# Building the place matrices of a PEER layer's gate stage on GpSimd instead of ScalarE

## The reference, cut to what matters

```python
act = jax.nn.gelu(jnp.einsum('thkd,td->thk', ub, xb), approximate=False)
vb = jnp.take(v, eb, axis=0)
return jnp.einsum('thk,thkd->td', gb * act, vb)
```

## Time and profile before

| what | value |
|---|---|
| time, median of 3 runs | 2997.28 us (2995.55 to 2999.19) |
| profiled execution, span from first to last instruction | 2998.2 us |
| profiled span against the median of the runs | 0.9 us longer |
| PE busy | 2734.9 us (91%) |
| DVE busy | 1819.1 us (61%) |
| ACT busy | 1457.1 us (49%) |
| POOL busy | 13.8 us (29 instructions) |
| mean granted TensorE clock | 0.94 of full speed |
| HBM traffic | 149 GB/s over the span |

### The profile page before, as it was taken

One profiled execution on the slowest core, in us unless ns is written; L12 is line 12 of the kernel. 1 busy time (PEld: TensorE's weight loads), 2 busy tenths in 40 slices (PEclk: granted clock), 3 DMA queues, 4 the chain that ended last, 5 costly groups with the idle time before them and its releaser, 6 DMA issues.

```text
span 2998.2 us, 47842 instructions
## 1 busy us (share of the span) xinstructions
PE 2734.9 (91%) x16426; PEld 2417.8 (81%) x16430; DVE 1819.1 (61%) x3134; ACT 1457.1 (49%) x2435; POOL 13.8 (0%) x29
## 2 busy tenths in 40 slices
PE   8889999977999997889999976899997998998898
PEld 6689999965888876579999965788876986866797
DVE  3456786499555553245778479655555656454564
ACT  4334444487454543334444477445444544553543
POOL 0000000000000000000000000000000000000000
PEclk9899999977999998789999987999998998998999
DMA  6245555500555553145555520455555554533454
GB/s 202 71 141 183 182 182 173 192 14 0 186 192 193 192 178 103 34 136 179 180 184 169 182 69 0 137 195 192 194 182 164 182 189 142 170 109 113 146 181 149
DMA packets 123982, 446.85 MB, mean 149 GB/s; under 512 B 14280, under 2 KB 14920, under 8 KB 123648
## 3 DMA queue, kind: packets, MB, share of 16 engines
q1 hardware_dynamic: 119808, 434.16, 44.0%
q0 software_dynamic: 2608, 9.08, 1.0%
q10 hardware_dynamic: 1488, 2.59, 0.2%
HBM read 444.74 MB, written 1.05 MB: 149 GB/s over the span
## 4 chain that ended last, share of the span: by engine, by line
PE 79%; DVE 13%; issue 4%; ACT 3%; DVEq 1%; DMA 0%; ACTq 0%
PE ps L621 38%; PE ps L593 12%; PE ps L599 12%; PE ps L596 12%; DVE SC L1750 3%; DVE big L1758 3%; DVE w_lo L337 1%; DVE SC L1400 1%; DVE X L1407 1%; DVEq L1750 1%; PE ps L571 1%; PE ps L818 1%; DVE tops L1694 1%; DVE big L1407 1%; DVE x_lo L1454 1%
## 5 line engine op out<-in xcount | busy, mean ns | idle before, releaser
L337 DVE TENSOR_TENSOR w_lo<-ring,w_hi 128x1024 fp32r<-128x1024 f32 (+1 forms) x808 | 986.2, 1221 | 917.8 <-ACT w_hi L330 907.0
L330 ACT CAST w_hi<-ring 128x1024 fp32r<-128x1024 f32 (+1 forms) x808 | 845.2, 1047 | 1115.8 <-PE ps L621 582.3
L593 PE MATMUL ps<-x_hi,w_hi 128*128 128x256 f32 x3136 | 775.4, 285 | 8.7 <-DVE x_lo L1459 4.4
L596 PE MATMUL ps<-x_lo,w_hi 128*128 128x256 f32 x3136 | 773.3, 284 | 0.0
L593 PEld LDWEIGHTS ps<-x_hi,w_hi 128*128 128x128 f32 x3136 | 605.0, 193 | 11.5 <-issue 10.4
L596 PEld LDWEIGHTS ps<-x_lo,w_hi 128*128 128x128 f32 x3136 | 605.3, 193 | 0.0
L599 PE MATMUL ps<-x_hi,w_lo 128*128 128x256 f32 x3136 | 443.3, 284 | 4.0 <-DVE w_lo L337 4.0
L621 PE MATMUL ps<-w_hi,x_hi 128*128 128x512 f32 x1488 | 417.8, 400 | 26.1 <-DVE x_lo L1454 12.6
L599 PEld LDWEIGHTS ps<-x_hi,w_lo 128*128 128x128 f32 x3136 | 405.7, 193 | 7.7 <-DVE w_lo L337 7.7
L621 PE MATMUL ps<-w_hi,x_lo 128*128 128x512 f32 x1488 | 409.8, 394 | 0.0
L621 PE MATMUL ps<-w_lo,x_hi 128*128 128x512 f32 x1488 | 407.9, 393 | 0.3 <-DVE w_lo L337 0.3
(11 more groups left out here) (221 smaller groups left out, 1512.5 us busy)
## 6 DMA issues: line engine op xcount, KB each, us to landing
ring<-in_u SPq DMA_DIRECT2D x256, 512.0 KB, 3.3
ring<-in_v SPq DMA_DIRECT2D x256, 512.0 KB, 3.2
ring<-in_ffn_in SPq DMA_DIRECT2D x88, 512.0 KB, 3.3
ring<-in_ffn_out SPq DMA_DIRECT2D x44, 512.0 KB, 3.3
ring<-in_wq SPq DMA_DIRECT2D x32, 512.0 KB, 3.3
ring<-in_ple_gate SPq DMA_DIRECT2D x16, 512.0 KB, 3.3
SC<-in_rows POOLq DMA_DIRECT2D x11, 512.0 KB, 4.4
ring<-in_a_qk SPq DMA_DIRECT2D x8, 512.0 KB, 4.5
```

Of the source, the lines that this page charges most:

```text
L330: nc.scalar.copy(part(w_hi, i)[:, used(name)], tile(i)[:, used(name)]).then_inc(tiles_hi, 1)
L337: nc.vector.tensor_tensor(part(w_lo, i)[:, at], tile(i)[:, at], part(w_hi, i)[:, at], ALU.subtract).then_inc(tiles_split, 1)
L593: mm = nc.tensor.matmul(bank(s)[:, 0:T], hi[:, k, :], x_hi[:, k, :], start=(k == 0), stop=False)
L596: nc.tensor.matmul(bank(s)[:, 0:T], hi[:, k, :], x_lo[:, k, :], start=False, stop=False)
```

## The change

GpSimd builds `place`, in a new function `places(layer)` in its own program. Two instructions do a group of four tokens: a subtraction with two inputs, `iota` repeated for each of four tokens and the four index columns repeated along 128 elements, into `distance` (128x512), and a comparison of that with zero into `place` (128x512). Between the two GpSimd waits on its own semaphore `distances`; from the fifth group on it waits for `slot_full` of group g - 4 ahead of the subtraction, as ACT did. `place` keeps its four buffers, its memory, and its values, zeros and ones. ACT's loop with five instructions per group is gone. `route_T[:, 1]` is now a plain copy of the index, where before it was multiplied by -1.

```diff
+            def places(layer):
+                gates = SLOT[f"gates{layer}"]
+                pool.wait_ge(routes_turned, layer + 1)
+                moved(pool, SLOT[f"last_u{layer}"], BODY)
+                for g in range(T // 4):
+                    k = g % 4
+                    if g >= 4:
+                        slot_here(pool, gates + g - 4)
+                    slots = route_T[:, 1, 4 * g:4 * g + 4]
+                    nc.gpsimd.tensor_tensor(distance[:, k], iota[:, None, :].to_broadcast([P, 4, P]),
+                                            slots[:, :, None].to_broadcast([P, 4, P]), ALU.subtract
+                                            ).then_inc(distances, 1)
+                    pool.wait_ge(distances, T // 4 * layer + g + 1)
+                    nc.gpsimd.tensor_scalar(place[:, k], distance[:, k], 0.0, None, ALU.is_equal
+                                            ).then_inc(place_rows, 1)
             load_rows(0, (gates_split, 1))
             load_rows(1, (routes_turned, 1))
+            places(0)
             load_p(0)
             load_rows(2)
             load_rows(3, (routes_turned, 2))
+            places(1)
             load_p(1)
...
-                def place_distances(k, turns):
-                    slot_here(act, gates + k - 4, turns)
-                    for t in range(4):
-                        ins = S.activation(distance[:, k, t], iota[:], ACT.Abs,
-                                           bias=route_T[:, 1, ds(turns * 16 + (4 * k + t), 1)])
-                    ins.then_inc(distances, 1)
-                def places(k, turns):
-                    act.wait_ge(distances, turns * 4 + (T // 4 * layer + k + 1))
-                    S.activation(place[:, k], distance[:, k], ACT.Relu, scale=-1.0, bias=1.0
-                                 ).then_inc(place_rows, 1)
...
                     if q == 0:
-                        ts(route_T[:, 1, :], bank(s)[:, T:2 * T], -1.0, None, ALU.mult)
+                        step(V.tensor_copy(route_T[:, 1, :], bank(s)[:, T:2 * T]))
```

## The result

The changed kernel takes 3041.94 us (median of 4 runs, 3041.5 to 3043.97) against 2996.5 us of the kernel before, timed beside it (4 runs, 2995.55 to 2999.19): 1.0158 times as long, 95% interval 1.0146 to 1.0171. It is slower, as forecast, but by 45 us and not by 188. One run of experiment 5 (3500.77 us) and one of experiment 7 (5338.7 us) were slow: their medians count them, their ratios don't.

The account below looks back on a forecast made before the run. DVE was taken to bound the gate stages at 2.23 us per group; 128 x (3.7 - 2.23) = +188 us took the span from 2998.2 to 3186, median 3185 us. Own range 3110 to 3265, 8-in-10 range 3015 to 3300.

Parts of the forecast that it names:

- What bounds the kernel before: Gate stages: DVE sets the pace at 2.23 us per group; removing ACT's 1.86 us gains nothing in the steady state.
- GpSimd's two instructions: Per group in the gate stages: subtraction 1.15, comparison 0.74, hop 0.13, alone 2.02 us, bounds 1.19 to 2.55.
- The step that failed: Gate stages: gate_group and GpSimd instructions exclude each other, apply_gates is free; 3.11 to 4.32 us per group, chance 0.63.
- The rule: Skill's shared-port rule for DVE and GpSimd in the gate stages: by it a group costs between 3.11 and 4.32 us.
- no exclusion, GpSimd too slow alone: Rival, gate stages: GpSimd's own cycle, at most 2.55 us, sets the pace; +41 us, 3038 us; chance 0.13.
- The signs that I had named: Gate stages, if right: apply_gates 3.1 to 4.3 us apart and unchanged in length, gate_group longer, PE waiting longer for gated_rows.
- The clock argument: Gate stages: PE's release starts the subtraction, beside gate_group at full clock, below apply_gates at lower clock; middle 3.7 us.
- The start of the stage: Before the first apply_gates: a faster first place could gain at most 3.3 us in both layers; first groups meet the block.
- The queues: GpSimd's in_p load stays at the stage's end, code readying hides behind the row loads, SP's queue is untouched: no cost.

Follow-up runs that it names:

- experiment 5: Changed kernel without the subtraction; GpSimd compares iota with each token's index column, four 128x128 comparisons per group: 3008.94 us, ratio 1.0034.
- experiment 7: Changed kernel with GpSimd's subtraction alone, no comparison, also waiting for DVE's gate_rows of group g-2: 3002.05 us, ratio 1.0025.
- experiment 8: Three-engine version of the changed kernel: GpSimd subtracts, lined up with apply_gates; ACT makes place and one weighted row of four, DVE three: 2968.29 us, ratio 0.9903.
- experiment 4: Changed kernel with a two-input product, distance times distance, in place of GpSimd's comparison: 3149.77 us, ratio 1.053.
- experiment 1: Changed kernel with one of DVE's four gate_group instructions per group, the other three left out: 3048.32 us, ratio 1.0187.
- experiment 2: Changed kernel with DVE's gate_group reading iota from a PSUM copy made once per layer: 3042.25 us, ratio 1.0169.
- experiment 6: Changed kernel with GpSimd's subtraction alone, written into place, no comparison, waiting only for PE's buffer: 3036.8 us, ratio 1.0135.

## Why the prediction was right in sign and wrong in size

- **What bounds the kernel before**: right. DVE at 2.23 us a group, and ACT's work off the path: with a quarter of `gate_group` off DVE the group takes 0.25 us less (experiment 8). No run takes ACT's work away and changes nothing else; in the changed kernel ACT idles, and nothing was gained.
- **GpSimd's two instructions**: the subtraction was 1.04 us for 1.15. The comparison was 1.49 us for 0.74, outside the bounds of 0.53 to 0.94: the rate of a memset says little about an instruction with another operation. The hops were 0.08 and none for 0.13. The sum alone was 2.58 us for 2.02, just above the upper bound of 2.55. The 2.6 cycles per element of the Trainium skill (GPSIMD Engine Reference, section 3.1) are near the subtraction (an estimate of 1.11 us for the measured 1.04). The 1.0 to 1.8 cycles that the prediction took from the same section of the Trainium skill for one input (1.03 for its leanest loops, about 1.8 as the best case of a tight one) are not near the comparison: 1.49 us for 512 elements are, by its 1.2 GHz, an estimated 3.5.
- **The step that failed** is "that a `gate_group` instruction and a GpSimd instruction exclude each other", taken for both of GpSimd's instructions, so that DVE's 1.02 us and all of GpSimd's work "must go one after another": 3.11 us a group at the least, 3.7 from the middle of its ends. It isn't the prices in that row that failed. With the measured 1.04 and 1.49 us its low end would be 3.75 us, and the group took 2.58. What the runs showed in its place: the exclusion holds in full for the subtraction (a `gate_group` instruction of 1.16 us beside it; 3.4 us a group on average with two such, experiment 4). The comparison holds up two instructions of four, so that it ran beside `gate_group` for a loss of 0.37 us. And in the steady state even that was not paid: as GpSimd itself was the slowest, it was never released by PE, and its subtraction came to lie at 703.52, below `apply_gates` at 703.19, where it blocks nothing. DVE's longer `gate_group` instructions fell into time that it would have waited (experiment 1). The pace was GpSimd's own 2.58 us, with the comparison at 1.49 us for 0.74.
- **The rule** of the Trainium skill (SBUF — State Buffer, Who interferes with whom) is that the first to issue has the shared ports for the whole instruction and the other is fully blocked. The rows agree for GpSimd's instruction with two inputs, though by its recorded start the held `gate_group` instruction (605.35) was ahead of the subtraction (605.39). They don't agree beside the comparison: of the three that meet it, one gets through in 0.33 us. By the same section a DVE instruction with at most one SBUF input outside the two-port modes doesn't contend with GpSimd; experiment 2, where the input lies in PSUM, agrees, with four `gate_group` instructions in 1.37 us.
- **The case that came true** is the rival "no exclusion, GpSimd too slow alone", with 3038 us at 2.55 us a group and a chance of 0.13. Its pace was right and half of its name: the exclusion was there. That the number fits so well is in part luck, since its terms were 1.35, 0.94 and 0.26 us and measured 1.04, 1.49 and 0.08. What it had for it, a middle only 0.2 us under the edge, deserved more: the sum of two unmeasured costs against a fixed 2.23 us. The signs that I had named don't tell the two cases apart: `gate_group` was longer (a mean of 527 ns for 331), `apply_gates` kept its length and PE waited for DVE rather than for `place`, all as under "Right"; the distance of 2.58 us alone spoke against the forecast.
- **The clock argument** used the right rows for a wrong end. PE fell to its lower level, and its group took 2.06 us, but the release by PE plays no part where GpSimd never waits for PE. Nor was PE idler with the longer groups: at the lower level it was busy for 80 of 100 us, where it had been for 71.
- **The start of the stage**: not the gain of up to 3.3 us that was open there, but a loss of 4.4 us in both layers, since the first twelve `gate_group` instructions met the block (7.01 and 7.00 us to the first `apply_gates`, for 4.95 and 4.63). Here the exclusion was paid, as the prediction had it for all groups.
- **The queues**: nothing there, as said. `in_p` is issued at the end of the stage, and the first subtraction starts with the last gelu.

## What to carry to other kernels

Moving work off an engine that isn't the bound gains nothing, and the engine that takes it must fit its whole cycle, hops included, below the bound's; here 2.58 against 2.23 us cost 45 us. When two engines fill exactly the same time, take away work from one of them to see which sets the pace, since the table of waits can't. Where GpSimd's two-input instructions run beside DVE instructions at the double rate, give GpSimd a wait that starts it with a DVE instruction it doesn't disturb: the same work then cost 6 us in place of 41, and the three-engine version gained 28 us with it and lost 10 without it.

## What the runs showed of the hardware that was not expected

- GpSimd's comparison of 128x512 with a constant takes 1.49 us, more than its subtraction of two inputs of the same size, 1.04 us; a comparison of 128x128 with a column takes 0.575 us.
- The subtraction holds up DVE's SBUF instructions at the double rate until its end (1.16 and 1.05 us for 331 ns). The comparison holds up those in its first 0.6 us and at its end (0.70 us each), and lets one between them pass (0.33 us).
- `apply_gates`, with one input in PSUM, keeps its length beside the two (a mean of 1.29 us before, 1.28 in the changed kernel, 1.31 in experiment 8).
- The same matmuls ran at a granted clock of 0.50 with a group each 2.58 us, 0.76 to 0.77 with one each 2.2 us, and 0.87 with one each 1.98 us. The length of a group alone doesn't tell it: it was 0.66 with 2.56 us (experiment 6) and 0.67 with 3.4 us (experiment 4).
